# Scores with half the rows for the keys' low part, later turned keys, x loaded first, another gate order

## The reference

```python
def layer(h, p):
    u = rmsnorm(h, mix_norm_g)
    q, k, v = split(u @ wqkv)                 # 16 / 4 / 4 heads of 64
    q, k = rmsnorm(q, gq), rmsnorm(k, gk)     # per head
    # blocks of 128 queries against the block before and their own
    scores = einsum('bnqkgd,bnskd->bnkgqs', qb, kb) * 64 ** -0.5
    scores = where(mask, scores - slopes * dist, -inf)
    m = maximum(scores.max(-1), sink)
    e = exp(scores - m)
    o = einsum('bnkgqs,bnskd->bnqkgd', e / (e.sum(-1) + exp(sink - m)), vb)
    h = h + o @ wo
    h = h + square(relu(rmsnorm(h, mlp_norm_g) @ w1)) @ w2
    gate = sigmoid(rmsnorm(h, ple_norm_g) @ w_gate)
    return h + gate * (p @ w_proj)
```

## Time and profile before

| | |
|---|---|
| Median of 3 runs | 1088.46 us (1087.74 to 1089.78) |
| The profiled execution | 1089.63 us, span 1087.9 us |
| TensorE matmul busy | 1061.6 us, 98% of the span, 4936 instructions |
| TensorE weight loads busy | 878.0 us, 81% |
| VectorE busy | 782.8 us, 72% |
| ScalarE busy | 472.2 us, 43% |
| GpSimd busy | 165.0 us, 15% |
| The chain that ended last | PE 80%, DVE 8%, POOL 4%, DMA 3%, issue 3%, ACT 3% |
| Scores (L2295) | 256 matmuls, 38.1 us busy |

### The profile page before, as it was taken

How to read it: one execution, slowest core, us unless ns; L and a number is a source line. 1 busy time by engine, 2 the same in 40 slices (tenths; PEclk the granted TensorE clock), 3 DMA queues, 4 the chain that set the end, 5 groups by cost and what they waited for, 6 DMA issues and landing times.

```text
span 1087.9 us, 14202 instructions
## 1 busy us (share of the span) xinstructions
PE 1061.6 (98%) x4936; PEld 878.0 (81%) x4936; DVE 782.8 (72%) x1127; ACT 472.2 (43%) x819; POOL 165.0 (15%) x277
## 2 busy tenths in 40 slices
PE   7899999999999999999999999999999999999998
PEld 6778887887888888888888888878888888888787
DVE  5877777778444499876676677476776878747985
ACT  5566666667433233313313233353333334437451
POOL 6765555544100000000000000000000000001000
PEclk8999999999999999999999999999999999999999
DMA  8111101131243307343253245998888998660102
GB/s 310 39 40 40 34 25 39 39 135 70 70 135 114 116 18 254 136 174 136 116 193 143 90 172 203 354 413 288 291 281 287 300 323 308 239 232 1 39 30 87
DMA packets 67756, 171.74 MB, mean 158 GB/s; under 512 B 5360, under 2 KB 5616, under 8 KB 67568
## 3 DMA queue, kind: packets, MB, share of 16 engines
q1 hardware_dynamic: 67264, 170.42, 43.7%
q10 hardware_dynamic: 432, 0.53, 0.1%
HBM read 133.18 MB, written 37.75 MB: 157 GB/s over the span
## 4 chain that ended last, share of the span: by engine, by line
PE 80%; DVE 8%; POOL 4%; DMA 3%; issue 3%; ACT 3%; SPq 0%; ACTq 0%; POOLq 0%; DVEq 0%
PE pair L2534 24%; PE pair L2514 24%; PE pair L2396 8%; PE pair L2261 6%; PE pair L2580 6%; PE pair L2472 3%; DMA wo_raw<-in_m_w 2%; PE pair L2608 2%; PE pair L2327 2%; PE pair L2295 1%; POOL q_rstd L811 1%; PE pair L2240 1%; PE pair L2442 1%; ACT probs L1050 1%; DVE probs L1631 1%
## 5 line engine op out<-in xcount | busy, mean ns | idle before, releaser
L2534 PE MATMUL pair<-uT 128*128 128x512 f32 x1344 | 306.0, 389 | 0.7 <-DVE uT L1964 0.7
L2534 PEld LDWEIGHTS pair<-uT 128*128 128x128 f32 x1344 | 252.0, 188 | 53.4 <-DVE uT L1964 1.2
L1309 ACT ACTIVATE uT<-wo_raw 128x1024 fp32r<-128x1024 f32 x83 | 84.7, 1054 | 113.9 <-PE pair L2534 97.2
L1964 DVE TENSOR_TENSOR uT<-wo_raw,uT 128x1024 fp32r<-128x1024 f32 x83 | 98.5, 1221 | 46.3 <-ACT uT L1309 46.0
L786 POOL TENSOR_SCALAR row_var<-row_ssq 128x1 f32<-128x1 f32 x16 | 4.0, 251 | 707.8 <-ACT hn L1350 624.7
L2396 PE MATMUL pair<-WA,oT 128*128 128x512 f32 x384 | 90.3, 392 | 0.6 <-DVE oT L1724 0.4
L2396 PEld LDWEIGHTS pair<-WA,oT 128*128 128x128 f32 x384 | 71.2, 188 | 15.9 <-issue 1.4
L2514 PE MATMUL pair<-WA,WB 128*128 128x512 f32 x336 | 78.2, 389 | 0.4 <-ACT xr L1284 0.4
L2514 PEld LDWEIGHTS pair<-WA,WB 128*128 128x128 f32 x336 | 63.0, 188 | 13.8 <-DVE WB L1898 0.8
L2580 PE MATMUL pair<-WA 128*128 128x512 f32 x288 | 68.4, 392 | 1.0 <-DVE WA L2155 1.0
L2580 PEld LDWEIGHTS pair<-WA 128*128 128x128 f32 x288 | 53.5, 188 | 12.7 <-DVE WA L2155 1.8
(11 more groups left out here) (242 smaller groups left out, 1884.2 us busy)
## 6 DMA issues: line engine op xcount, KB each, us to landing
wo_raw<-in_m_w SPq DMA_DIRECT2D x71, 512.0 KB, 6.5
wo_raw<-hid_kept SPq DMA_DIRECT2D x41, 512.0 KB, 5.9
hid_kept<-RES SPq DMA_DIRECT2D x32, 512.0 KB, 2.8
emb<-in_m_w SPq DMA_DIRECT2D x17, 512.0 KB, 6.3
RES<-in_m_w SPq DMA_DIRECT2D x8, 1024.0 KB, 7.1
uT_f<-in_m_w SPq DMA_DIRECT2D x6, 1024.0 KB, 6.8
RES<-in_a_wqkv SPq DMA_DIRECT2D x10, 512.0 KB, 9.2
emb<-hid_kept SPq DMA_DIRECT2D x10, 512.0 KB, 5.9
```

The lines of the kernel that those rows point to most:

```text
L1309: nc.scalar.activation(operand(t, which, HI), unit(t, which), ACT.Copy).then_inc(op_hi, 1)
L1964: nc.vector.tensor_tensor(operand(t, which, LO), unit(t, which), operand(t, which, HI).bitcast(F32), ALU.subtract).then_inc(op_ready, 1)
L2534: mm = nc.tensor.matmul(ps[4 * (j % 2) + m][:], operand(t, 0, s)[:, k, m * P:(m + 1) * P], operand(t, 1, r)[:, k, :], start=(g == 0 and k ...
```

## The change

It does seven things.

1. **Scores.** k's low part is now multiplied by q's high part alone, with the 64 rows that hold it, so that even heads use rows 0 to 63 and odd heads rows 64 to 127. The matmuls of an even and an odd head stand side by side: high, high, low, low, for each of two pairs. Even heads go to one bank and odd heads to the other. The product of the two low parts falls away. VectorE's copies span both banks, so each of the two waits for the whole call.
2. **Turned keys.** At the end of a block, q8 is projected over k tiles 0 to 3 ahead of turn_k instead of 0 and 1.
3. **First block.** The last eight matmuls of q8's first projection come behind scores(0, 0) instead of ahead of it.
4. **x first.** SP issues xt's two halves ahead of the weights, and x_turned is laid out block by block in memory. xb comes after five weight units, not four.
5. **ScalarE at the start** splits weight unit 0 before the second half of xT.
6. **GpSimd at the start** scales block 1's x before x_norm(0) and head_norm("k", 0), no longer after all the first bias rows.
7. **Gate.** TensorE: embed(0), turn_d(5), P1's last tile, embed(1), turn_d(6), P2's first tiles, with turn_d(7) in the middle of P2's second. ScalarE splits S1 after gate(1), VectorE takes S1's low part ahead of S3.

```diff
@@ SP
+            sp.dma_start(xt[:, 0:4, :], x_turned[0, :, 0:4, :]).then_inc(xt_first, 16)
+            sp.dma_start(xt[:, 4:8, :], x_turned[0, :, 4:8, :]).then_inc(xt_in, 16)
             for u in range(U_W1):
-                if u == 4:
+                if u == 5:
                     sp.dma_start(xb[:], x[0:P, :]).then_inc(x_in, 16)
@@ ScalarE
-            act.dma_start(xt[:, 0:4, :], x_turned[:, 0, 0:4, :]).then_inc(xt_first, 16)
-            act.dma_start(xt[:, 4:8, :], x_turned[:, 0, 4:8, :]).then_inc(xt_in, 16)
...
             gate(1)
+            gate_hi_part("S1")
             gate(2)
             gate(3)
-            gate_hi_part("S1")
@@ VectorE, add_bias
-                    stand(dve, scores_ready, 2 * t + (1 + half_bank))
-                    nc.vector.copy_predicated(score_keys[half_bank][:, :, 0, :],
+                    stand(dve, scores_ready, 2 * t + 2)
+                    nc.vector.copy_predicated(score_keys[:, :, half_bank, 0, :],
@@ VectorE, gate
             add_gated(0)
             add_gated(1)
+            gate_lo_part("S1")
             form("S3_first")
             form("S3")
-            gate_lo_part("S1")
@@ TensorE, scores
-                for r in range(G):
-                    dst = score_bank[r // 2][:, (r % 2) * 2 * P:(r % 2 + 1) * 2 * P]
+                for h in range(G // 2):
                     for m in (HI, LO):
-                        mm = nc.tensor.matmul(dst, qT[:, G * j + r, :], kT[:, m, j, :, :].rearrange("p a n -> p (a n)"),
-                                              start=(m == HI), stop=(m == LO))
-                    if r % 2 == 1:
-                        mm.then_inc(scores_ready, 1)
+                        for odd in range(2):
+                            rows = slice(0, P) if m == HI else q_rows(odd, HI)
+                            mm = nc.tensor.matmul(score_bank[odd][:, h * 2 * P:(h + 1) * 2 * P], qT[rows, G * j + 2 * h + odd, :],
+                                                  kT[rows, m, j, :, :].rearrange("p a n -> p (a n)"),
+                                                  start=(m == HI), stop=(m == LO))
+                            if (h, m) == (1, LO):
+                                mm.then_inc(scores_ready, 1)
@@ TensorE, body
                     if j == 3 and not last:
                         turn_q("q0", n + 1)
-                        project("q8", n + 1, 1 - par, kts=range(0, 2))
+                        project("q8", n + 1, 1 - par, kts=range(0, 4))
                         turn_k(n + 1, 1 - par)
-                        project("q8", n + 1, 1 - par, kts=range(2, Q8_TAIL[0]))
+                        project("q8", n + 1, 1 - par, kts=range(4, Q8_TAIL[0]))
```

More of the change, by code:

```diff
@@ L387, in trunk_layer @@
         score_bank = (ps[2], ps[3])
-        score_keys = [bank.rearrange("p (h a n) -> p h a n", h=2, a=2) for bank in score_bank]
+        score_keys = pair[1][:].rearrange("p b (h a n) -> p b h a n", h=2, a=2)
         pT_bank = (ps[4], ps[5])
@@ L583, in load_xt @@
                 sp.wait_ge(xT_ready, b + 1)
-                sp.dma_start(xt[:], x_turned[:, bass.ds(b, 1)].rearrange("p b k n -> p (b k) n")).then_inc(xt_in, 16)
+                sp.dma_start(xt[:], x_turned[bass.ds(b, 1)].rearrange("b p k n -> p (b k) n")).then_inc(xt_in, 16)
             def load_xb(b):
@@ L845, in _ @@
                 if h == 11:
+                    scale_x(1)
                     x_norm(0)
@@ L911, in body @@
                 mask_probs(4 * n + 2)
-            scale_x(1)
             pool.wait_ge(consts_in, 16)
@@ L1163, in _ @@
             first_xT_hi(0)
+            hi_unit(0, "kv", 0)
             first_xT_hi(1)
-            hi_unit(0, "kv", 0)
             hi_unit(1, "kv", 1)
@@ L1598, in add_bias @@
                 for half_bank in range(2):
-                    stand(dve, scores_ready, 2 * t + (1 + half_bank))
-                    nc.vector.copy_predicated(score_keys[half_bank][:, :, 0, :],
+                    stand(dve, scores_ready, 2 * t + 2)
+                    nc.vector.copy_predicated(score_keys[:, :, half_bank, 0, :],
                                               current[:].bitcast(U32).unsqueeze(1).to_broadcast([P, 2, P]),
-                                              score_keys[half_bank][:, :, 1, :]).then_inc(wrapped, 1)
+                                              score_keys[:, :, half_bank, 1, :]).then_inc(wrapped, 1)
                 for r in range(G):
@@ L1614, in add_bias @@
                     nc.vector.tensor_tensor_reduce(
-                        probs[:, i, r, 0:P], score_keys[r // 2][:, r % 2, 0, :],
+                        probs[:, i, r, 0:P], score_keys[:, r % 2, r // 2, 0, :],
                         bias[:, G * j + r, :], 1.0, 0.0, ALU.add, ALU.max, rmax[:, i, r:r + 1]).then_inc(biased, 1)
@@ L2340, in body @@
                     if j == 0 and not last:
-                        if not first:
+                        if first:
+                            project_first("q8", (HI, 3), (LO, 2), (LO, 3))
+                        else:
                             project("q8", n, par, kts=Q8_TAIL)
@@ L2414, in _ @@
             turn_q("q0", 0)
-            project_first("q8", (HI, 3), (LO, 2), (LO, 3))
             body(0, 0, first=True)
@@ L2560, in _, with gate @@
                     turn_d((t - (STEPS - 6)) // 2)
-            def gate(name, m):
+            def gate(name, m, ks=range(4)):
                 _, left, right = [x for x in GATE_PRODUCTS if x[0] == name][0]
@@ L2577, in gate @@
                     pe.wait_ge(z_added, logits_added(1, m))
-                for k in range(4):
+                for k in ks:
                     for q, (u, r) in enumerate(PASSES):
@@ L2583, in gate @@
                                               stop=(name in ("P2", "P3", "P4") and k == 3 and q == 2), skip_group_check=True)
-                mm.then_inc(gate_done, 1)
+                if ks[-1] == 3:
+                    mm.then_inc(gate_done, 1)
             def embed(s):
@@ L2617, in _ @@
             gate("P1", 2)
+            embed(0)
+            turn_d(5)
             gate("P1", 3)
-            turn_d(5)
+            embed(1)
+            turn_d(6)
             gate("P2", 0)
[L2621 to L2624, removed]
+            gate("P2", 1, ks=range(0, 2))
             turn_d(7)
+            gate("P2", 1, ks=range(2, 4))
             gate("P2", 2)
@@ L2653 @@
     laid = {"x": x,
-            "x_turned": x.reshape(blocks, P, tiles, P).transpose(3, 0, 2, 1),
+            "x_turned": x.reshape(blocks, P, tiles, P).transpose(0, 3, 2, 1),
             "p_turned": p.reshape(p.shape[0], p.shape[1] // P, P).transpose(2, 1, 0),
```

## The result

The changed kernel takes **1102.38 us** (median of 4 runs, 1101.7 to 1102.8), the kernel before 1088.81 beside it: a ratio of 1.0125, 95% interval 1.0113 to 1.0137. It is slower by 13.6 us. The forecast was 1084.3, in a range of 1081 to 1094. The profiled execution took 1101.7 with a span of 1100.0, 12.1 above the span before.

What follows compares the result with a forecast made beforehand. TensorE's matmul stream was taken as the bound, 98% of the span. Terms 2.85 - 0.25 + 2c + 5 x (2c - 0.85) + 4c = -1.65 + 16c gave -4.15 us at c = -0.156: 1088.46 to 1084.3, range 1081 to 1094.

Steps and rivals of the forecast that it cites:

- Scores: Attention scores: half-row low passes of even and odd heads overlap in part, making each call of eight matmuls 0.156 us shorter.
- c: What one scores call (eight matmuls, four heads) costs more than before; taken as -0.156 us.
- the switch: In the scores: going between full-row and half-row matmuls, four times a call; up to 0.153 us each, left out of the forecast.
- the other end: Scores with each switch costing 153 ns: c = +0.35 us with overlap, +0.61 without.
- the nearer row: Profile row of four transposes, 0.09 us each, read as weight loading; it gave the scores c = -0.156.
- the prediction's own formula: For blocks 1 to 5: 5 x (2c + the larger of -0.85 and -1.39 + 2c); blocks 0, 6 and 7 2c each.
- The rival "the switch costs": Scores: switches between row forms make c = +0.35, the sum +4.8 us, 1093.3 in all; chance 0.24.
- Turned keys: End of a block: later turn_k saves 0.85 us a block, with a new 0.5 wait at the scores; block 6 gains nothing.
- Start: First block: GpSimd waits for block 1's x, landing at 20.2, so turn_k(0) comes 2.85 us later.
- The tail of q8: First block: q8's last eight matmuls behind the first scores, taking 1.83 us, delay the next projection by 0.6.
- Gate: Gate: the 1.03 us wait for S1 goes and 1.2 appears at the next product; taken as zero, bounds -1.2 and +0.5.
- VectorE's wait for the whole call: Scores: VectorE's first copy waits for all eight matmuls; covered in the loop, 0.5 us without that cover.

Runs made afterwards that it cites:

- e2: The kernel before with only the scores' part of the change (half rows, banks by parity, VectorE's copies over both banks): 1096.11 us, ratio 1.0068.
- e9: e3 with all four low passes on rows 0 to 63, so the odd heads' correction is wrong: 1099.39 us in one run.
- e3: The changed kernel with a call's four full passes first, then its four half-row passes, two changes of row use instead of four: 1092.14 us, ratio 1.003.
- e6: The changed kernel with all rows in the low passes and GpSimd's scale_x(1) back behind block 0's norms and the bias rows: 1081.97 us, ratio 0.994.
- e12: e8 with the last eight matmuls of q8's first projection again ahead of block 0's first scores: 1079.48 us, ratio 0.9917.
- e8: e6 with the gate's order of the kernel before on all three engines: 1081.13 us, ratio 0.9933.
- e11: e3 with the half-row passes issued twice over, so k's low part is added twice: 1096.79 us in one run.
- e5: e3 with the four low passes in the order even, even, odd, odd: 1093.23 us in one run.
- e4: The changed kernel with each head's low pass right behind its high pass, eight changes of row use a call: 1135.04 us in one run.

## Why the prediction was wrong

**Scores: the step that failed.** The prediction took c = -0.156, from transposes that load weights and do overlap, and counted the switch at nothing. It is +0.55. The overlap itself is the full one (0.24 a call, where I took 0.156 of 0.258), so that half was too small, not too large. The switch (my word there for a change of row use) was in the text as the other end, 0.153 each, worked out from the length of a record; the runs give 0.195. I took the value that the nearer row favoured, though that row has no change of form in it and so could say nothing of the term that decides. With the measured price the prediction's own formula gives for blocks 1 to 5: 5 x (1.10 - 0.29) = 4.05, measured 4.2; for block 6 1.1, measured 1.1; in all +9.95. One count in it is not borne out: in e2 block 0 does not grow at all at c = +0.55, where the formula has 2c. The rival "the switch costs" was the right mechanism with too small a price: 1093.3 foretold for c = +0.35.

The Trainium skill, TensorEngine Tiling (Array Packing), section Key Properties, says that a change of tiling mode drains TensorE, and that different tiles can work in parallel. The runs agree as far as they can show it: a change costs 0.19 to 0.20 us, though no row shows that it is a drain, and a call takes 1.31 us with the low passes on the same half (e9) and 1.08 on different halves (e3).

**Turned keys: right.** Foretold 0.85 us a block. Without the half rows (e6) blocks 1 to 5 take 147.19 us against 151.41, 0.84 a block. The new wait for kT is there too:

```profile
177.32 0.60 PE L2308 MATMUL pair<-ident,probs 128*128 128x128 f32 x4
178.15 1.21 PE L2296 MATMUL pair<-kT,qT 128*128 128x256 f32 x8 [0.23 <-DVE kT L1564]
```

The idle time in brackets counts from the end of the record, and four transposes are shown with 0.60 us but take 0.35 from start to start. So the scores come 178.15 - 177.32 - 0.35 = 0.48 us late, which is the foretold 0.5. In the changed kernel it doesn't show, because TensorE is the later one: a block grows by 4 x 0.55 - 1.39 = 0.81, so all four calls lie on the path. One point was wrong: block 6 gains as well, 30.52 us in e6 against 31.61 before, 1.1 us that I had denied. So the keys are worth 6.1 in all and not 5.1.

**Start: the mechanism right, the size off.** Foretold +2.85 at turn_k(0), measured +4.4. The link that was off is the landing of block 1's x: I had it at 20.2 "again", with the same bytes ahead of it in the queue. But before, x of block 0 came through ScalarE's queue, and now its 512 KB go through SP's, ahead of the weights. The load of block 1's x was issued at 10.9 instead of 10.3 and took 10.7 instead of 9.9:

```profile
L584 SPq DMA_DIRECT2D xt<-in_x_turned x7: 332/333/1162, 10.9 to 185.7; - x7
...
DMA to landing us min/median/max: 3.2/3.4/10.7
```

That is 1.4 later; from there on the chain is the foretold one (scaling 1.9, x_rstd at 24.4, the unit, eight matmuls at half clock in 3.6). The 10.7 comes with SP's new order: all twelve traces with it have 10.7, and the two without it (before and e2) 9.9 and 9.5. The issue time says little, as it lies anywhere from 10.2 to 11.6 in the twelve. That x's bytes in the queue are the cause fits, but was not tried. e6 confirms the whole term: without the wait, turn_k(0) is 3.2 before the old time.

**The tail of q8: undersized.** Foretold +0.6, with the eight matmuls at full clock. The pause of 2.34 us that they used to fill in part is now open, the clock falls behind it, and they take 3.5 us in the changed kernel. e12 against e8 puts a price of 1.65 us on the edit (1.0 between the profiled executions). I had this very effect in the sum one step earlier, at the pause of the weights, and did not ask for it here.

**Gate: the bound, not the zero.** P5's wait went and 1.2 us stand at P6, as foretold. The cost is at my bound of +0.5 (0.54 in the traces of e6 and e8, 0.8 between their medians, 0.4 in the changed kernel). It comes from VectorE, which waits 0.95 for ScalarE's half of S1. I had looked at ScalarE's side of that edit, not at VectorE's.

**VectorE's wait for the whole call: covered**, as foretold. TensorE's wait for rmax is 1.3 us as before, and e6, in which VectorE does wait for whole calls (twice, 0.4 us in all), still gains 0.84 a block.

**From -4.15 to 12.1:** the scores at their measured price 14.1 (up to 9.95), the landing of x 1.55, block 0 with the tail 0.7 (what its calls add and what the tail adds are not separated), blocks 1 to 6 0.15, the gate 0.4, block 7 0.7 less than foretold (0.4, not 1.1). The measured 13.6 between the medians holds 1.5 us that are not of this ledger: the profiled execution of before lies 0.8 above its median, that of after 0.7 below.

## What to carry to other kernels

Before you use half-row matmuls, count the changes of row use, not the matmuls: a change costs 0.195 us here and a pair on both halves saves 0.12, so there must be more than 2 x 0.195 / 0.12 = 3.25 pairs between going to half rows and coming back, and this call had one (two in e3). e11 has four: with the 0.10 behind, its twelve matmuls take 1.41 us, where twelve full ones would take about 1.03 + 4 x 0.12 = 1.51 (an estimate). Work that filled a wait on TensorE also held its clock here (e12), so moving it out of the wait was paid twice. An operation that waits for a transfer must not be put ahead of a small one that another engine waits for.

## What the runs showed that I had not expected

- The four half-row matmuls overlap also when the program has them even, even, odd, odd (e5 and e3: call 1.08), and the trace shows them started in another order than the program's.
- The length of a record doesn't tell what a matmul costs. The half-row ones of the changed kernel are shown with 0.38 us, where full ones had 0.28. But in e4, where none has a partner, it is 0.38 too, and in e3 it is 0.38 for the first pair behind the change and 0.28 for the second. The longer record goes with the change of row use, not with running side by side.
- The price of a change doesn't depend on their number: 2, 4 and 8 a call give 0.195, 0.20 and 0.19 us. In e4, where every matmul changes the form, the row runs at 0.31 us a matmul instead of 0.12.
- It is the same in both directions, and half of it stands behind the change. In e3 the starts are 166.16 (last full matmul), 166.37 and 166.59 (the two pairs), 166.80 (the next group, full): 0.21, 0.22, 0.21, and 0.10 too much behind it. Against steps of 0.12 that is 0.09 + 0.10 for going in and 0.09 + 0.10 for coming back. So the changed kernel's call hides a fifth of its loss (0.10 of 0.55), which stands in the group behind.
